# Another order of the latent attention loop in a two-layer hybrid step on one core

## The reference

```python
def block(q_blk):
    s = jnp.einsum('bqgrd,bkgd->bgrqk', q_blk, k).astype(jnp.float32) * scale
    p = jax.nn.softmax(s, axis=-1).astype(v.dtype)
    return jnp.einsum('bgrqk,bkgd->bqgrd', p, v)
```

## Time and profile before

| | us |
|---|---|
| median of three runs | 1917.44 |
| lowest and highest | 1916.29, 1919.79 |
| the profiled execution | 1921.2 |
| its span, first to last instruction | 1919.4 |

### The profile page before, as it was taken

One profiled execution on the slowest core, in us unless ns is written; L12 is line 12 of the kernel. 1 busy time (PEld: TensorE's weight loads), 2 busy tenths in 40 slices (PEclk: granted clock), 3 DMA queues, 4 the chain that ended last, 5 costly groups with the idle time before them and its releaser, 6 DMA issues.

```text
span 1919.4 us, 31024 instructions
## 1 busy us (share of the span) xinstructions
PE 1778.9 (93%) x12114; PEld 1615.6 (84%) x12114; DVE 949.7 (49%) x1382; ACT 591.9 (31%) x952; POOL 135.3 (7%) x76
## 2 busy tenths in 40 slices
PE   4999987998999999999989997889989999999997
PEld 3888865568999999999978886645979999999996
DVE  4433256544665256445653314565456644553665
ACT  2511214332643133223352112343254422331331
POOL 0100003430000000000001000234000000000000
PEclk8999987899899999999989998889989999999997
DMA  8445400002233322422224542000212222222222
GB/s 311 151 132 182 140 12 1 1 23 67 88 88 118 114 76 66 132 60 66 72 97 134 169 162 66 1 0 1 67 37 74 87 71 70 79 86 68 66 66 66
DMA packets 170201, 161.44 MB, mean 84 GB/s; under 512 B 10500, under 2 KB 154876, under 8 KB 169980
## 3 DMA queue, kind: packets, MB, share of 16 engines
q1 hardware_dynamic: 167804, 151.75, 24.9%
q0 software_dynamic: 2304, 8.39, 1.2%
HBM read 156.96 MB, written 3.15 MB: 83 GB/s over the span
## 4 chain that ended last, share of the span: by engine, by line
PE 61%; issue 27%; DVE 7%; DMA 2%; ACT 1%; SPq 1%; POOL 0%; DVEq 0%; POOLq 0%; ACTq 0%
PE psum L510 61%; DMA m_stage<-in_w_mod_dram 1%; DMA m_pre_b<-in_w_mod_dram 1%; DVE mx_a L1711 1%; DVE ret_st L1660 1%; SPq L411 1%; DVE mx_b L1713 0%; DVE w_lo L1458 0%; DVE a_dec L1640 0%; DVE y_t L1891 0%; DVE rows L1895 0%; DVE ql_odd L1700 0%; DMA w_stage<-in_w_out_dram 0%; DVE acc L1723 0%; ACT w_hi L1177 0%
## 5 line engine op out<-in xcount | busy, mean ns | idle before, releaser
L510 PE MATMUL psum<-act_hi,w_hi 128*128 128x320 f32 x2048 | 475.6, 314 | 18.8 <-DVE act_lo L1484 16.8
L510 PE MATMUL psum<-act_lo,w_hi 128*128 128x320 f32 x2048 | 469.9, 311 | 0.0
L510 PE MATMUL psum<-act_hi,w_lo 128*128 128x320 f32 x2048 | 469.8, 311 | 0.0
L510 PEld LDWEIGHTS psum<-act_hi,w_hi 128*128 128x128 f32 x2048 | 344.5, 190 | 27.9 <-issue 25.9
L510 PEld LDWEIGHTS psum<-act_lo,w_hi 128*128 128x128 f32 x2048 | 346.3, 190 | 0.0
L510 PEld LDWEIGHTS psum<-act_hi,w_lo 128*128 128x128 f32 x2048 | 345.2, 189 | 0.0
L1458 DVE TENSOR_TENSOR w_lo<-w_stage,w_hi 128x1024 fp32r<-128x1024 f32 x200 | 233.3, 1204 | 95.7 <-ACT w_hi L1177 88.8
L1177 ACT ACTIVATE w_hi<-w_stage 128x1024 fp32r<-128x1024 f32 (+1 forms) x196 | 194.2, 1033 | 215.8 <-PE psum L510 152.2
L510 PE MATMUL psum<-g_hi,w_hi 128*128 128x320 f32 x704 | 162.2, 311 | 6.5 <-DVE g_lo L1869 6.5
L1827 DVE SCALAR_TENSOR_TENSOR x<-psum,mod,x 128x128 f32 (+5 forms) x192 | 72.8, 434 | 184.6 <-PE psum L510 183.4
L510 PE MATMUL psum<-g_lo,w_hi 128*128 128x320 f32 x704 | 161.5, 310 | 0.0
(11 more groups left out here) (245 smaller groups left out, 2057.0 us busy)
## 6 DMA issues: line engine op xcount, KB each, us to landing
w_stage<-in_w_up_dram SPq DMA_DIRECT2D x176, 256.0 KB, 3.7
m_stage<-in_w_mod_dram SPq DMA_DIRECT2D x64, 512.0 KB, 4.7
w_stage<-in_w_down_dram SPq DMA_DIRECT2D x80, 256.0 KB, 3.3
w_stage<-in_w_in_dram SPq DMA_DIRECT2D x72, 256.0 KB, 5.4
w_stage<-in_w_out_dram SPq DMA_DIRECT2D x32, 256.0 KB, 3.0
m_next<-in_w_mod_dram POOLq DMA_DIRECT2D x16, 512.0 KB, 5.5
m_pre_a<-in_w_mod_dram SPq DMA_DIRECT2D x10, 512.0 KB, 13.4
w_stage<-in_dft_dram SPq DMA_DIRECT2D x16, 256.0 KB, 4.6
```

The costliest lines, as they stand in the source:

```text
L510: return pe.matmul(out, lhs, rhs, start=start, stop=stop, skip_group_check=True)
```

## The change

The order of the loop is written anew on PE and on DVE. Score step 0 of a pass moves into the pass itself, with value product 5 of the pass before between its high and its low part. The maxima stand in steps 0 to 4 (12 in five steps), where before they reached to the end of step 5. Both row turns come ahead of the last value product of the pass, behind value product 3 and behind score step 5. The sums stand behind score step 2, and the spread behind score step 3. On DVE the subtractions of `rest_q` go from behind maximum 1 to behind maximum 11. `mx_a` and `mx_b` become one tile, `mx_ab`, with the two halves of a maximum side by side, and the fold becomes a reduce over them.

```diff
-        mx_a = sb("mx_a", [P, 2, 8], F32, phase)
-        mx_b = sb("mx_b", [P, 2, 8], F32, phase)
+        mx_ab = sb("mx_ab", [P, 2, 8, 2], F32, phase)
...
-                scores_hi(0, 0)
-                scores_lo(0, 0)
                 for t in range(4):
...
+                    scores_hi(t, 0)
+                    if t:
+                        values(t - 1, 5)
+                    scores_lo(t, 0)
+                    next_max(0, 1)
                     scores_hi(t, 1)
                     scores_lo(t, 1)
-                    next_max(0, 1)
+                    next_max(2, 3)
                     values(t, 0)
+                    next_max(4)
+                    scores_hi(t, 2)
+                    scores_lo(t, 2)
                     if t:
                         sums(t - 1)
-                    next_max(2)
-                    scores_hi(t, 2)
-                    scores_lo(t, 2)
-                    next_max(3)
+                    next_max(5)
                     values(t, 1)
+                    next_max(6, 7)
+                    scores_hi(t, 3)
+                    scores_lo(t, 3)
+                    next_max(8)
                     if t:
                         spread_inverses(t - 1)
-                    next_max(4, 5)
-                    scores_hi(t, 3)
-                    scores_lo(t, 3)
-                    next_max(6)
                     values(t, 2)
-                    next_max(7)
+                    next_max(9, 10)
                     scores_hi(t, 4)
                     scores_lo(t, 4)
+                    next_max(11)
+                    values(t, 3)
                     if more:
                         max_rows(t + 1, 0)
-                    next_max(8)
-                    values(t, 3)
-                    next_max(9)
                     scores_hi(t, 5)
                     scores_lo(t, 5)
-                    next_max(10)
+                    if more:
+                        max_rows(t + 1, 1)
                     values(t, 4)
-                    next_max(11)
-                    if more:
-                        scores_hi(t + 1, 0)
-                        max_rows(t + 1, 1)
-                        values(t, 5)
-                        scores_lo(t + 1, 0)
                 values(3, 5)
...
-                        dve.tensor_tensor(mx[:, t % 2, 4 * e:4 * e + 4], mx_a[:, t % 2, 4 * e:4 * e + 4],
-                                          mx_b[:, t % 2, 4 * e:4 * e + 4], ALU.max).then_inc(mc_ok, 1)
+                        dve.reduce_max(mx[:, t % 2, 4 * e:4 * e + 4], mx_ab[:, t % 2, 4 * e:4 * e + 4, :], AX.X).then_inc(mc_ok, 1)
...
                     if more:
-                        rest_q(t + 1)
-                        maxima(t + 1, 2)
+                        maxima(t + 1, 2, 3, 4)
                     if t:
                         inverse(t - 1)
                     if more:
-                        maxima(t + 1, 3, 4)
+                        maxima(t + 1, 5, 6, 7, 8)
                     if t:
                         normalised_output(t - 1)
                     if more:
-                        maxima(t + 1, 5, 6)
+                        maxima(t + 1, 9, 10, 11)
+                        rest_q(t + 1)
                     if t:
                         rest_output(t - 1)
-                    if more:
-                        maxima(t + 1, *range(7, 12))
```

More of the change, by code:

```diff
@@ L1710, in maximum @@
                     if m % 3 < 2:
-                        dve.reduce_max(mx_a[:, t % 2, at + m % 3:at + m % 3 + 1], src, AX.X).then_inc(mx_ok, 1)
+                        dve.reduce_max(mx_ab[:, t % 2, at + m % 3, 0:1], src, AX.X).then_inc(mx_ok, 1)
                     else:
-                        dve.reduce_max(mx_b[:, t % 2, at:at + 2], src.rearrange("p (b n) -> p b n", b=2), AX.X).then_inc(mx_ok, 1)
+                        dve.reduce_max(mx_ab[:, t % 2, at:at + 2, 1], src.rearrange("p (b n) -> p b n", b=2), AX.X).then_inc(mx_ok, 1)
                     if m == 5:
                         dve.wait_ge(mx_ok, 48 * L + 12 * t + n + 1)
-                        dve.tensor_tensor(mx[:, t % 2, 4 * e:4 * e + 4], mx_a[:, t % 2, 4 * e:4 * e + 4],
-                                          mx_b[:, t % 2, 4 * e:4 * e + 4], ALU.max).then_inc(mc_ok, 1)
+                        dve.reduce_max(mx[:, t % 2, 4 * e:4 * e + 4], mx_ab[:, t % 2, 4 * e:4 * e + 4, :], AX.X).then_inc(mc_ok, 1)
                 def last_sum(t):
```

## The result

The changed kernel takes 1894.03 us (median of four executions, 1893.01 to 1901.58), the kernel before 1918.25 in the same comparison: a ratio of 0.9875, with a 95% interval of 0.9857 to 0.9893. That is 24.2 us less (interval 20.5 to 27.4). The forecast was 17.7 us less, 1899.7, in a range of 1893 to 1912. A later comparison gave 1899.01 to 1920.10, ratio 0.9884 (0.9857 to 0.9910), 21.1 us less.

The account below looks back on a forecast made before the run. The kernel was taken as bound by the order and clock of PE's matmuls. Idle time 11.5 us plus clock 6.2 gave 17.7 us saved, 1917.4 to 1899.7 us, in a range of 1893 to 1912.

Parts of the forecast that it names:

- Idle time: PE's gaps in the attention loop's passes: 12.7 us go, 1.2 come back ahead of maximum 4, 11.5 us saved.
- The caught last sum: Rival: DVE's last sum is held behind POOL's first add in four passes; 1918.4 us, no change; chance 0.07.
- Fold: The two folds ahead of each loop, now reduces, cost 0.1 us on PE's path, at worst 2.0.
- Clock: PE in the loops: three 3.4 us stretches at half clock in place of seven, 6.2 us saved.
- The price: One 3.4 us stretch of PE at half clock costs a pass 1.55 us.
- The rate of one in two: Half of the six passes that hold sums would have a half-clock stretch, so three.
- No falls at all: Rival: PE's loops keep full clock without waits, 22.4 us saved, 1895.1 us; chance 0.16.
- Two falls at each sums: Rival: the sums themselves bring two half-clock stretches in each of six passes, 3.8 us saved, 1913.7 us; chance 0.10.
- falls at the small matmuls of every step: Rival (slower): sums, spread and turns each drop PE's clock, 18 half-clock stretches, 5.5 us lost, 1923.0 us; chance 0.05.

Follow-up runs that it names:

- the subtraction put back: Changed kernel with rest_q moved back behind the last sum, ahead of maximum 2: 1925.36 us, ratio 1.0034.
- One sum of eight: One of the sums' eight products issued in passes 1 to 3: 1885.56 us in the changed kernel, 1906.91 us in the kernel before.
- the sums twice: Changed kernel with the same eight products of the sums issued twice in passes 1 to 3: 1917.41 us, ratio 0.9984.
- the sums behind value product 0: Changed kernel with the sums put back directly behind value product 0, ahead of score step 2: 1902.12 us, ratio 0.9911.
- maximum 2 first: Changed kernel with maximum 2 ahead of the last sum on DVE: 1896.10 us, ratio 0.9880.
- three gaps closed: Changed kernel with maximum 2 ahead of the last sum, pass 3's sums ahead of value product 0, and rest_q(0) later ahead of the loop: 1890.29 us.
- its repeat: Kernel before, run once more without an edit: 1914.92 us, one execution.
- the subtractions alone: Kernel before with only rest_q on DVE moved from behind the last sum to behind maximum 11: 1912.89 us, ratio 0.9969.
- the run with halves: Changed kernel with four sums behind value product 0, four behind value product 1, and DVE's inverse behind the reduce of maximum 5: 1896.15 us.
- the last run: Changed kernel with sums in halves, pass 3's first half ahead of value product 0, and rest_q(0) late ahead of the loop: 1884.30 us.

## Why the prediction was right, and where it was short

**Idle time: right, to the tenth.** Every gap that was to go is gone, every one that was to stay has stayed (0.77 in pass 3), and the new one is 0.35 in pass 1 and 0.22 in pass 2, where 0.3 was charged. Between the two profiled executions 11.6 us of gaps went, 11.5 were forecast. The subtractions are covered as worked out: held to 2.76 and 2.77, with no gap behind them. The caught last sum did not come: the add begins 0.95 after it. The rule of the Trainium skill (SBUF — State Buffer, "Who interferes with whom") holds in all traces here; in the two loops, a subtraction that begins while an add of POOL runs ends behind that add and takes 2.40 to 2.88, 80 times in 14 traces; the 88 others take 0.67 to 0.69. With the subtraction put back, the gap ahead of maximum 4 is 3.68.

**Fold: right.** 0.16, no cost.

**Clock: the forecast held, in part by luck; one side of the term was mis-sized.** Three falls were forecast in the passes; two traces of the change have two and five. The price holds: 22.41 against 20.79, less 0.13 of gap, is 1.49; 1.55 was taken. The rate of one in two was read from two passes 3 alone, and it came out: six of the twelve passes with sums fell in these two traces. From two cases, that is luck. Mis-sized are the falls of the kernel before: seven were taken from one trace, and the second has ten.

**What sets the falls off.** The prediction saw gaps and sums stand together in passes 1 and 2 and could not tell what each does. The runs can. One sum of eight keeps the gaps, and none of passes 1 to 3 falls, in either order; with the sums twice each of them falls. So these falls need the sums, and the gaps of 0.2 to 1.2 do not bring them alone. A gap is not needed either: of 14 passes in which the sums stand in one block and PE has no gap near them (the sums behind value product 0, maximum 2 first, three gaps closed), six fell. That gaps close to the sums make the falls surer is what the counts say: all twelve passes 1 and 2 fell in three traces of the before order (the first, its repeat, the subtractions alone), five of eight in the change. No run takes the gap of 1.00 away and leaves the rest, so it is not shown. The long gaps are another matter: in or at most 1.3 us behind each of the eight gaps of 3.43 to 3.68 in the passes of all traces a fall begins, before any sums.

**Where the other 6 us came from.** The sum was made from one execution, and that was a favourable one of the kernel before: a gap of 1.01 in its first pass 0 and seven falls, where the second has 3.43 and ten. From the first exp to the end the two loops take 174.1 and 177.9 us in these two, 153.6 and 157.5 in two of the change: means 20.5 apart, 2.8 more than forecast. As an estimate, 1.2 of that is the gap (the mean of 1.01 and 3.43 in place of 1.01) and 1.5 is one fall more (from 8.5 to 3.5 on the mean, where seven to three was taken). The rest, to 24.2 or 21.1, lies within the intervals of the comparisons. Falls outside the loops, which the change does not touch, move single executions by more than that: the two traces of the kernel before have 185 and 164 us at low clock in the whole span (mean clock 0.952 and 0.957), of which 26 and 34 lie in the passes. Which falls the timed executions had, no trace shows; that part stays open.

**Rivals.** No falls at all did not happen in a trace of the change. Its best timed executions, 1893.0 to 1894.3 at a mean clock of 0.959, lie below that rival's 1895.1, but where their falls lay is not on record. The rule of the Trainium skill behind this rival (TensorE: Matmul & The Clock Gate, "HAM oscillation — how this bites in real kernels") would have an order without gaps keep the full clock; here it did not: pass 2 of the run with maximum 2 first fell with PE busy for all of its 22.02. For the gaps of 3.43 to 3.68, each with a fall, the traces agree with it. Two falls at each sums did not come; one of twelve passes had two. Nor did falls at the small matmuls of every step: no fall in the passes follows a row turn or the spread without the sums ahead of it in either trace of the changed order.

## What to carry to other kernels

Read the granted clock of a stretch beside its gaps, and beside what PE is busy with: here 16 one-column matmuls in one block behind a gap of 1 us went with one or two falls in all of twelve passes, at about 1.55 us each, and without any gap with a fall in six of 14. When one instruction of an engine in order can be held by another engine, place it where its reader is farthest, not where it is ready first; the subtraction that POOL holds takes 2.8 in both places, and in the changed kernel it costs 3.3 of PE's idle time in the one and nothing in the other. And when a sum is made from one execution, look at a second one for the waits that are decided by a tenth of a microsecond.

## What the runs showed that was not expected

* PE's clock fell to 1.2 GHz while PE was busy without a gap: behind the 16 one-column matmuls of the sums, 1.8 us in one block. The same 16 in two blocks, with dense matmuls between and no gap beside them, brought no fall in ten passes of two traces (passes 1 and 2 of the run with halves, passes 1 to 3 of the last run). In one block without a gap they brought one in six of 14.
* The combination matters: value product 0 behind a gap of 0.77, with sums right behind it, fell for 10.2 us in four of four passes 3, whether all of the sums stood there or half of them; with a score step between, in the two traces of the change, it fell in one of four. In the before order, where a row turn stands closer ahead of the pair and the spread one score step sooner behind it, it fell for 3.4 us in four of six passes 3. What sets the length is open.
* A gap of 3.68 in place of 0.35, with the same sums behind it, took 6.5 us more from pass 1 and not 3.3: 28.89 against 22.41. The rest goes with two falls more.
